# The output projection's third token tile: its matmuls after each half's eight chunks instead of after every second chunk

## What is computed

```python
def token_mixer(xn, ...):
    z = xn @ w_in                     # q and kv latents, rotary key, B, C, h
    ...                               # 8 heads of latent attention -> attn
    ...                               # gated causal convolution    -> conv_out
    y = jnp.concatenate([rmsnorm(attn, g_ao), rmsnorm(conv_out, g_co)], axis=-1) @ w_o
    return y, c_kv, k_rope, u_ext[:, -(CONV_W - 1):]

def trunk_layer(x, ...):
    mix, c_kv, k_rope, new_conv = token_mixer(rmsnorm(x, norm_mix), ...)
    h = x + mix
    ffn = hier_moe(rmsnorm(h, norm_ffn).reshape(B * T, D), ...)   # 32 experts, top-1 group, top-2 in it
    return h + ffn, c_kv, k_rope, new_conv
```

## Time and profile before

| | |
|---|---|
| runs | 1610.18, 1612.42, 1615.23 us, median 1612.42 |
| span of the profiled execution (first to last instruction) | 1613.5 us |
| its time beside the span | not given by the page; the median of the runs is 1.1 us below this span |
| TensorE busy | 1272.8 us |
| VectorE, ScalarE busy | 393.7 us, 378.5 us |
| mean granted TensorE clock | 0.896 |
| output projection on TensorE | from about 420 to 560 us of the span |

### The profile page before, as it was taken

The page is one execution under the profiler, slowest core; times in us unless marked ns, Lnnn a source line. Parts: engine busy times, 40 slices in busy tenths (PEclk is TensorE's granted clock), DMA queues, the critical chain, the costliest instruction groups (busy, mean ns, idle before and its releaser), DMA issues.

```text
span 1613.5 us, 19649 instructions
## 1 busy us (share of the span) xinstructions
PE 1272.8 (79%) x7570; PEld 655.1 (41%) x7571; DVE 393.7 (24%) x737; ACT 378.5 (23%) x643; POOL 31.9 (2%) x41
## 2 busy tenths in 40 slices
PE   5999999999899996677677677568678666766765
PEld 4999998566566641221122122122122112212212
DVE  6354443245554330120120120120113012012013
ACT  5333322143433221112112112112120111211213
POOL 1001000001000000000000000000000000000000
PEclk9999999999899988888878889879897888988987
DMA  9444540123433389999989999999976998999993
GB/s 322 140 144 154 157 138 33 37 81 107 129 125 106 130 338 420 420 374 420 421 363 422 421 373 420 421 406 390 420 293 247 420 421 366 421 420 384 422 420 139
DMA packets 110801, 475.38 MB, mean 295 GB/s; under 512 B 14156, under 2 KB 51136, under 8 KB 60304
## 3 DMA queue, kind: packets, MB, share of 16 engines
q1 hardware_dynamic: 109776, 470.86, 73.3%
q0 software_dynamic: 832, 2.48, 0.4%
q10 hardware_dynamic: 64, 0.02, 0.0%
HBM read 469.96 MB, written 3.38 MB: 293 GB/s over the span
## 4 chain that ended last, share of the span: by engine, by line
PE 61%; DMA 26%; issue 7%; DVE 2%; ACT 1%; SPq 1%; ACTq 0%; DVEq 0%
DMA ring<-in_w_up 14%; PE ps L843 12%; DMA ring<-in_w_down 11%; PE ps L871 7%; PE ps L574 5%; PE ps L575 5%; PE ps L576 5%; PE ps L858 5%; PE ps L822 3%; PE ps L746 2%; PE ps L635 2%; PE ps L662 2%; PE ps L755 2%; PE ps L748 2%; PE ps L747 2%
## 5 line engine op out<-in xcount | busy, mean ns | idle before, releaser
L843 PE MATMUL ps<-ring,mix 128*32 128x512 f32 x2112 | 335.6, 772 | 242.9 <-issue 131.6
L843 PEld LDWEIGHTS ps<-ring,mix 128*32 128x32 f32 x2112 | 75.3, 131 | 495.7 <-issue 322.0
L1533 DVE TENSOR_TENSOR mix<-mix,ps 128x128 f32<-128x128 f32 x33 | 9.5, 288 | 765.5 <-ACT mix L1166 765.5
L1163 ACT COPY mix<-ps 128x512 f32<-128x512 f32 x33 | 35.5, 1076 | 616.0 <-PE ps L843 616.0
L574 PE MATMUL ps<-xT_hi,w_hi 128*128 128x320 f32 (+1 forms) x528 | 165.8, 314 | 3.9 <-DVE work L1258 3.9
L575 PE MATMUL ps<-xT_lo,w_hi 128*128 128x320 f32 (+1 forms) x528 | 164.8, 312 | 0.0
L576 PE MATMUL ps<-xT_hi,w_lo 128*128 128x320 f32 (+1 forms) x528 | 164.6, 312 | 0.0
L858 PE MATMUL ps<-ring,mix 128*32 128x512 f32 x1056 | 122.3, 596 | 29.4 <-DVE mix L1533 17.6
L871 PE MATMUL ps<-mix 128*128 128x512 f32 (+1 forms) x192 | 99.6, 678 | 23.9 <-ACT mix L1171 23.1
L822 PE MATMUL ps<-r,work 128*32 128x512 f32 (+1 forms) x816 | 107.9, 616 | 0.4 <-DVE work L1516 0.2
L1272 DVE TENSOR_TENSOR w_lo<-ring,w_hi 128x1024 fp32r<-128x1024 f32 (+1 forms) x66 | 76.8, 1205 | 117.3 <-ACT w_hi L978 117.3
(11 more groups left out here) (259 smaller groups left out, 1117.4 us busy)
## 6 DMA issues: line engine op xcount, KB each, us to landing
ring<-in_w_gate SPq DMA_DIRECT2D x128, 1024.0 KB, 20.7
ring<-in_w_up SPq DMA_DIRECT2D x128, 1024.0 KB, 22.8
ring<-in_w_down SPq DMA_DIRECT2D x128, 1024.0 KB, 23.6
ring<-in_w_in SPq DMA_DIRECT2D x32, 1024.0 KB, 8.1
ring<-in_w_o SPq DMA_DIRECT2D x16, 1024.0 KB, 6.2
hreg<-in_x_prompt SPq DMA_DIRECT2D x4, 1024.0 KB, 6.1
ring<-in_w_uq SPq DMA_DIRECT2D x4, 768.0 KB, 4.9
ring<-in_w_uv SPq DMA_DIRECT2D x2, 1024.0 KB, 5.9
```

What stands on the lines that cost most here:

```text
L843: last = pe.matmul(ps[r:r + B, 2, :], x[:, c + o, s, :], w[:, m, c + o, :], start=s == 0 and c == 0, stop=s == 3 and c == 2)
```

## The change

The third tile's matmuls leave the loop over the eight chunks of a half and form a loop of their own behind it. Each chunk's result goes to the same partitions as before.

```diff
@@ output(n)
                         if j % 2 and not final:
                             last.then_inc(o_used, 1)
-                        if j % 2:
-                            for k in range(2):
-                                last = pe.matmul(b[2][64 * k:64 * k + 64, :], mix[:, c - 1 + k, 256:320], w[:, j - 1 + k, :],
-                                                 start=half == 0 and j == 1, stop=final)
-                            if final:
-                                last.then_inc(psum_full, 1)
-                            elif j == 7:
-                                last.then_inc(wo_half_used, 1)
+                    for j in range(8):
+                        k = j % 2
+                        last = pe.matmul(b[2][64 * k:64 * k + 64, :], mix[:, 8 * (1 - half) + j, 256:320], w[:, j, :],
+                                         start=half == 0 and j < 2, stop=half == 1 and j > 5)
+                    last.then_inc(psum_full if half else wo_half_used, 1)
```

## The result

The changed kernel takes 1602.03 us (median of 7 runs, 1595.91 to 1609.68) and the kernel before 1610.97 us (7 runs, 1607.87 to 1615.44): a ratio of 0.9944, 95% interval 0.9920 to 0.9968. On another chip (six runs beside fourteen of the kernel before) it was 0.9924 (0.9901 to 0.9948). So about 9 us are gained (5 to 13 by the interval). The profiled execution of the changed kernel took 1609.68 us with a span of 1607.5; it is the longest of the seven, which the last part of "Why" comes back to.

A forecast was written before the change was run, and what follows sets the result against it. TensorE was taken to bound the output projection; 8.6 us for 24 removed turns plus 0.8 for a wait make 9.4 us, from the median 1612.4 to 1603.0 us, range 1598.8 to 1608.5.

The forecast's parts named there:

- What bounds it: Output projection: TensorE works 54.65 of 55.4 us, so time saved there shortens the path if operands arrive.
- The price of a turn: Output projection: switching to third-tile matmuls and back costs time above their work; 24 of 32 switches go, saving 8.6 us.
- 0.36 us: Cost of one switch to third-tile matmuls and back in the output projection, above the work itself; lower bound 0.32 us.
- The wait: First block, between halves: line 746's 0.83 us wait for m_lo goes, 9.85 us of work covering a 9.3 us chain.
- The sum: Whole kernel: 8.6 + 0.8 = 9.4 us off, 1603.0 us from the median of 1612.4.
- What is late next: Output projection: split W_o chunks still arrive in time, no stall; DVE's additions starting some 2.6 us sooner gain nothing.
- load-bound batch: Third-tile batch: weight loads don't lie under matmuls, a batch takes 4.48 us, the kernel 1610.6 us; chance 0.10.
- The rule: Third-tile batch: a load overlaps only a matmul using different row groups, making inner steps 0.564 us; the forecast didn't follow it.
- The clock stayed at 1.00 in the batch: Against the rival that the granted clock falls in third-tile batches, some 3.4 us more each, 1630 us; chance 0.04.
- hidden downstream: Expert stage: it waits for DMA, so the output projection's gain doesn't show, 1612 us; chance 0.06.
- The spread: Output projection and after: clock falls may come elsewhere, 4.2 us either way, plus about 1.3 us run spread above.

The follow-up runs named there:

- 16 turns: Third-tile matmuls behind every fourth chunk, four at a time, instead of behind every second as in the kernel before; median 1605.64 us, ratio 0.9941.
- full-width kernels: Third-tile matmuls given 128 array columns instead of 64, in the order of before and of the change; 1631.15 and 1627.59 us, beside 1619.3 before.
- kernel with the old first half: The changed kernel, but the first half of the first block keeps the old order; 1604.62 us in one run, beside 1619.3 before.
- four turns: All 16 third-tile matmuls of a block behind its second half, against eight behind each half in the change; median 1606.76 us, ratio 0.9942.
- batch of four even and four odd chunks: The changed kernel with the even chunks first in each batch, then the odd ones; 1618.95 us in one run, beside 1619.3 before.

## Why the prediction held

*What bounds it.* Shown: 9.6 us less in TensorE's output projection are about 9 us less in the time. That the stretch from the stage's end to the first expert matmul stayed at 27.4 us is in part chance: it was 28.4 us in the changed kernel's second profile, and from 24.6 (16 turns) to 28.4 us over the ten profiles.

*The price of a turn.* The mechanism held, the size was a little small: the term "0.36 us" measured 0.384 (a half went from 15.84 to 14.69 us, 1.15 us for three turns), above the 0.37 that I got with 0.2275 us for the whole run. The long run goes at 0.2272 us a step; of the first steps after a turn I had counted too little as the turn's. So 24 turns are 9.2 us, not 8.6. I had left open whether the cut or the format makes the price; by the full-width kernels the format alone makes about a sixth of it. With this agrees the Trainium skill, "TensorEngine Tiling (Array Packing)", section "Key Properties": a change of the tiling mode drains TensorE. The runs give 0.38 us for a change there and back, format included.

*The wait.* 0.83 us gone, as in the sum; the chain of 9.3 us against 9.69 us of work (9.85 was predicted), so 0.4 us to spare and not 0.55. Line 582 came 2.04 us earlier in the stage (7.79 us behind its start instead of 9.83), not 2.4. The kernel with the old first half brings it back.

*The sum.* 9.2 + 0.83 is 10.0 us, and the stage in the two profiled executions shows 9.6. Most of the other 0.4 us is the clock. The stage opens at the lower of the clock's two levels (1.2 GHz of 1.2 and 2.4; a mean of 0.55 granted in its first 4.6 us before, 0.50 behind the change), and the first twelve matmuls took 4.53 us before and 4.79 behind the change, from the first start to the twelfth:

```profile
420.27 0.79 PE L746 MATMUL ps<-o_hi,m_hi 128*128 128x512 f32 x1
...
424.80 0.40 PE L748 MATMUL ps<-o_hi,m_lo 128*128 128x512 f32 x1
...
418.50 0.79 PE L746 MATMUL ps<-o_hi,m_hi 128*128 128x512 f32 x1
...
423.29 0.39 PE L748 MATMUL ps<-o_hi,m_lo 128*128 128x512 f32 x1
```

In each execution the clock also fell once behind a router call. Before, the run of twelve there took 4.19 us instead of 2.95, and the router call 0.3 us more: 1.5 us. Behind the change, the run of 48 took 12.73 us instead of 11.10: 1.6 us (1.3 was predicted for a fall). So the predicted 9.4 us lie close to the 9.6 because a turn counted too cheap and a clock that took more behind the change nearly cancel. That the time came within 1 us of the forecast (1602.0 against 1603.0) is luck as well: the interval of the gain is 8 us wide, and the median of the kernel before fell from 1612.4 to 1611.0 us with the four further runs.

*What is late next.* No matmul of line 746 waits for `o_lo` in a run, with 48 or with 96 matmuls in it. DVE's earlier start brought nothing, as costed: the router's transpose of the third tile stands 8.3 us behind the stage's end in both (568.71 less 560.43, 557.37 less 549.05).

*The rivals.* The load-bound batch is refuted: it lasts 3.58 us, not 4.48, so the weight loads lie under the matmuls. The rule of the Trainium skill, "TensorE: Matmul & The Clock Gate", section "The mechanism", that loads overlap only where the row groups differ, doesn't hold for these rows; the same section also lets a load run ahead into a background weight buffer, and with that the rows agree, though no run here shows the buffer itself. The clock stayed at 1.00 in the batch, and all eight last 3.58 or 3.59 us. The gain wasn't hidden downstream: the medians show it.

*The spread.* The profiled execution of the change has the same rows from the first expert matmul on as the one before, and took 1031.0 us there (576.46 to 1607.5) instead of 1025.7 (587.79 to 1613.5). Over the ten profiles of this study that part lasts from 1021.2 (four turns) to 1031.0 us with no order in the turns; why is not shown. So one execution's span shows 6 us of gain (9.6 in the stage and 1.8 ahead of it, less 5.3 behind) and the medians show 9, and kernels 1 us apart can't be told apart by time.

## What to carry to other kernels

Look in the order of time for steps that are longer where the work changes its form; where such a change is paid each time, collect the work of one form, as far as a wait or a buffer allows. Then count what the collected block covers: the batch between the halves hid a wait, and the kernel that went on to four turns lost that cover, and with it more than the fewer turns brought. Keep neighbours that run side by side together when the work is moved.

## What the runs showed of the hardware that was not expected

A change of number format alone is nearly free, 0.06 to 0.07 us for a turn in the full-width kernels. Around line 582 in the changed kernel a float32r matmul, two fp32 records of 320 columns and another float32r matmul take 1.00 us (426.06 to 427.06), as much as their own steps (2 x 0.23 + 2 x 0.27, the latter 320 columns at the 0.43 us of 512).

Matmuls of the other half of the array's columns don't keep strictly to their place in the list. In the batch of four even and four odd chunks about half of the pairs overlapped (5.42 us instead of about 7.1), so odd ones ran beside even ones that stand up to some four records ahead of them. Its weight loads stand one at a time from 435.61 to 436.46 us, two or three at a time from 436.89 to 437.75, and one at a time again from 438.24. "TensorE: Matmul & The Clock Gate" of the Trainium skill, section "The mechanism", has matmuls start and end in program order; this batch's length does not fit a strict order of the starts. How far ahead TensorE looks wasn't tried.
